# Feed-forward by Strassen's seven products in a split-precision decoder kernel

## The reference, cut to what matters

```python
h = h + jnp.einsum('btnd,de->bte', g * pb, w_out)
u = rmsnorm(h, g_mlp) @ w_up
h = h + jnp.square(jax.nn.relu(u)) @ w_down
h = h + (p_l @ w_ple) * jax.nn.sigmoid(rmsnorm(h, g_ple) @ w_ple_gate)
```

## Time and profile before

| | us |
|---|---|
| median of 3 runs | 2022.32 |
| lowest, highest | 2021.87, 2022.51 |
| span of the profiled execution | 2021.3 |
| product with w_out and feed-forward, in the chain | 1061.4 to 1878.7 |

### The profile page before, as it was taken

How to read it: one execution, slowest core, us unless ns; L and a number is a source line. 1 busy time by engine, 2 the same in 40 slices (tenths; PEclk the granted TensorE clock), 3 DMA queues, 4 the chain that set the end, 5 groups by cost and what they waited for, 6 DMA issues and landing times. The chain is left out here.

```text
span 2021.3 us, 34022 instructions
## 1 busy us (share of the span) xinstructions
PE 1994.1 (99%) x12822; PEld 1961.5 (97%) x12822; DVE 874.8 (43%) x1359; ACT 438.3 (22%) x855; POOL 637.1 (32%) x414
## 2 busy tenths in 40 slices
PE   8999999999999999999999999999999999999997
PEld 7999999999999999999999999999999999999997
DVE  5101443447464655544675543123213311444557
ACT  5112333321111222231232221012002200212312
POOL 2323222222232222224473233232323232323423
PEclk9999999999999999999999999999999999999999
DMA  3441212126443555587553111111111111111313
GB/s 117 136 137 32 57 54 63 58 79 198 121 141 116 172 152 162 164 163 225 179 175 102 53 42 51 43 46 48 44 50 42 52 42 52 42 52 42 105 32 126
DMA packets 239738, 190.35 MB, mean 94 GB/s; under 512 B 17005, under 2 KB 209625, under 8 KB 239268
## 3 DMA queue, kind: packets, MB, share of 16 engines
q1 hardware_dynamic: 224004, 167.03, 28.5%
q10 hardware_dynamic: 15648, 22.13, 3.5%
HBM read 156.05 MB, written 33.09 MB: 94 GB/s over the span
## 5 line engine op out<-in xcount | busy, mean ns | idle before, releaser
L142 PE MATMUL acc<-x_hi,w_hi 128*128 128x344 f32 x2448 | 791.7, 323 | 1.2 <-DVEq L1794 1.2
L142 PE MATMUL acc<-x_hi,w_lo 128*128 128x344 f32 x2448 | 782.8, 320 | 0.0
L142 PE MATMUL acc<-x_lo,w_hi 128*128 128x344 f32 x2448 | 782.0, 319 | 0.0
L112 POOL TENSOR_SCALAR w_hi<-w_raw 128x1024 fp32r<-128x1024 f32 (+1 forms) x174 | 182.0, 1046 | 1176.4 <-PE acc L142 991.5
L142 PEld LDWEIGHTS acc<-x_hi,w_hi 128*128 128x128 f32 x2448 | 460.9, 188 | 2.3 <-issue 1.5
L142 PEld LDWEIGHTS acc<-x_lo,w_hi 128*128 128x128 f32 x2448 | 460.6, 188 | 0.0
L142 PEld LDWEIGHTS acc<-x_hi,w_lo 128*128 128x128 f32 x2448 | 460.5, 188 | 0.0
L115 POOL TENSOR_TENSOR w_lo<-w_raw,w_hi 128x1024 fp32r<-128x1024 f32 (+1 forms) x174 | 407.0, 2339 | 14.5
L142 PE MATMUL acc<-z_hi,w_hi 128*128 128x344 f32 x768 | 246.0, 320 | 0.0
L142 PE MATMUL acc<-z_lo,w_hi 128*128 128x344 f32 x768 | 245.0, 319 | 0.0
L142 PE MATMUL acc<-z_hi,w_lo 128*128 128x344 f32 x768 | 245.0, 319 | 0.0
(11 more groups left out here) (307 smaller groups left out, 2110.1 us busy)
## 6 DMA issues: line engine op xcount, KB each, us to landing
w_raw<-in_w_in SPq DMA_DIRECT2D x64, 512.0 KB, 4.2
page<-in_cache_k SPq DMA_DIRECT2D x64, 256.0 KB, 3.1
page<-in_cache_v SPq DMA_DIRECT2D x64, 256.0 KB, 2.7
w_raw<-in_w_up SPq DMA_DIRECT2D x32, 512.0 KB, 4.0
w_raw<-in_w_down SPq DMA_DIRECT2D x32, 512.0 KB, 4.1
merge_gate<-merge_gates SPq DMA_DIRECT2D x22, 516.0 KB, 3.7
merge_gates<-gate_out ACTq DMA_DIRECT2D x18, 516.0 KB, 3.3
w_raw<-in_w_ple_gate SPq DMA_DIRECT2D x14, 512.0 KB, 4.2
```

Source lines behind the costliest of these rows:

```text
L112: nc.gpsimd.tensor_scalar(k.w_hi[:, par, 0:kb, :], k.w_raw[:, par, 0:kb, :], 1.0, 1.0, ALU.mult, ALU.mult).then_inc(k.w_rounded, 1)
L142: mm = k.nc.tensor.matmul(k.acc[:, c, 0:CW], w[:, par, i, :], x[:, i, cols], start=(i == 0 and j == 0), stop=(i == kb - 1 and j == 2))
```

## The change

The feed-forward's two products are made by Strassen's scheme in its Winograd form. An up *pair* is two blocks of 128 outputs, the two halves of the contraction (even and odd blocks of h) and two halves of 516 columns (`HALF`), each half as two units of 258 (`UNIT`). Seven products replace eight. In a product of an up pair 2 units x 4 tiles x 3 passes = 24 matmuls run; a down pair takes only 4 blocks of u (`DOWN_GROUPS` = 8 groups of 4 pairs), so its products have 12. Seven of the sums that the scheme needs are accumulated in PSUM or added by VectorE.

The operands are new: for the weights GpSimd makes four sums per pair, ScalarE rounds the seven operands (before, GpSimd did), GpSimd makes their low parts. For z the sums are made once (`t_mix`, `t_hi`, `t_lo`); for u per up pair: three quadrants are read and gated with two instructions each, one with one, then squared, four differences are made, and seven operands rounded and split. They are stored in DRAM (`u_rows`) from a buffer of 4 slots in h's upper half and loaded again for the down products; h itself goes to DRAM (`h_back`) and comes back. The sums of squares are multiplied by ones between the first and the second product of pair 0.

```diff
+PRODUCTS = (1, 5, 6, 2, 7, 3, 4)
+    def round_weight(self, act, pair, o):
...
+            act.wait_ge(s["product"], pair.n * NPROD + (o - 2 if o < 3 else -1 if o == 3 else o - 3))
+        k.nc.scalar.activation(self.slot(pair, o, k.w_hi), self.weight_source(pair, o), ACT.Copy).then_inc(s["w_hi"], 1)
+    def split_pair(self, pool, pair):
...
+        nc.gpsimd.tensor_tensor(t0, a21, a22, ALU.add).then_inc(s["sums_ready"], 1)
...
+        nc.gpsimd.tensor_tensor(t1, t0, a11, ALU.subtract).then_inc(s["sums_ready"], 1)
+        for o in range(4):
+            low(o)
+        pool.wait_ge(s["w_lo"], pair.n * NPROD + 2)
+        nc.gpsimd.tensor_tensor(t0, a11, a21, ALU.subtract).then_inc(s["sums_ready"], 1)
+        low(4)
+        pool.wait_ge(s["w_lo"], pair.n * NPROD + 3)
+        nc.gpsimd.tensor_tensor(t1, a12, t1, ALU.subtract).then_inc(s["sums_ready"], 1)
+        low(5)
+        low(6)
+    def multiply(self, pe, pair, o, tiles):
+        pe.wait_ge(s["w_lo"], pair.n * NPROD + o + 1)
+        if j == 2:
+            pe.wait_ge(s["p1"], pair.n + 1)
...
+            pe.wait_ge(s["read"], pair.n * READS + {1: -3, 5: -1, 6: 0, 7: 2, 3: 1, 4: 4}[j])
+        for e in range(2):
+            for i, (b, kt) in enumerate(tiles):
+                hi, lo = (self.ops.rows(j, b, part, kt)[:, 0, e * UNIT:(e + 1) * UNIT] for part in range(2))
+                for step, (w, x) in enumerate(((w_hi, hi), (w_hi, lo), (w_lo, hi))):
...
+    def scalar(self, act):
+        def steady(pair, after):
+            n = pair.n
+            square(n - 1, 3, 2)
+            u_hi(n - 1, 2)
+            self.round_weight(act, pair, 3)
+            keep_p1(n)
+            u_hi(n - 1, 3)
+            self.round_weight(act, pair, 4)
+            u_hi(n - 1, 4)
+            self.round_weight(act, pair, 5)
+            u_hi(n - 1, 5)
+            self.round_weight(act, pair, 6)
+            square(n, 0, 0)
+            u_hi(n - 1, 6)
+            self.round_weight(act, after, 0)
+            square(n, 1, 3)
+            u_hi(n, 0)
+            self.round_weight(act, after, 1)
+            square(n, 2, 1)
+            u_hi(n, 1)
+            self.round_weight(act, after, 2)
...
+    def vector(self, dve):
+        def open_other(n, o, j, other, quad, right, i):
+            dve.wait_ge(s["product"], n * NPROD + o)
+            nc.vector.tensor_tensor(two_units(quads[:, quad, :]), self.read_bank(j), two_units(other), ALU.add)\
+              .then_inc(s["read"], 1)
+            dve.wait_ge(s["read"], n * READS + i + 3)
+            nc.vector.scalar_tensor_tensor(out=quads[:, quad, :], in0=quads[:, quad, :], scalar=0.0,
+                                           in1=rstd[:, token_half(right)], op0=ALU.max, op1=ALU.mult).then_inc(s["opened"], 1)
...
+        def steady(n):
+            open_21(n - 1)
+            mixed(n - 1, 0)
+            mixed(n - 1, 1)
+            u_lo(n - 1, 2)
+            mixed(n - 1, 2)
+            keep_f(n)
+            u_lo(n - 1, 3)
+            keep_u2(n)
+            u_lo(n - 1, 4)
+            open_11(n)
+            u_lo(n - 1, 5)
+            mixed(n - 1, 3)
+            open_22(n)
+            u_lo(n - 1, 6)
+            u_lo(n, 0)
+            open_12(n)
+            u_lo(n, 1)
...
+        def down_pair(pair, previous, extra):
...
+            previous()
...
+            keep_f(n)
+            add_kept(n, 2 * q + 1, 0, P1)
...
+            keep_u2(n)
...
+            add_kept(n, 2 * q + 1, 1, F)
...
+            add_read(n, 4, 2, 2 * q, 0)
...
+            add_kept(n, 2 * q, 1, U2)
...
+            add_read(n, 5, 7, 2 * q + 1, 1)
...
+            add_read(n, 6, 3, 2 * q, 1)
@@ MixOut.sync, for b in range(3, KD) @@
             weights(b)
+            store(b - 3)
@@ Merge.gpsimd, for q in range(NQ) @@
+            if q == KD:
+                pool.wait_ge(k.mlstm_done, 1)
+                k.clear_semaphores(pool, k.decode_sems)
+@@ back_half, sync @@
+            sp.wait_ge(done["product"], ALL * NPROD)
+            sp.wait_ge(done["sq_added"], 4 * OUTS)
```

More of the change, by code:

```diff
@@ L1607 @@
 NQ = len(STEPS)
-BLOCK_PARTS = [(b, slice(0, TT)) for b in range(KD - 1)] + [(KD - 1, cols) for cols in CHUNKS]
-NP = len(BLOCK_PARTS)
 class Merge:
@@ L1934, in back_half @@
[L1934 to L1940 removed]
+        plain_place = ctx.enter_context(ExitStack())
@@ L1953, in back_half @@
         sent = [k.sem(ctx, f"y_sent{i}") for i in range(3)]
-        last = {n: k.sem(ctx, "ld_" + n) for n in ("h_done", "rounded", "split", "squared", "sq_added")}
-        PG = KD * NCH
+        ffn = FeedForward(k, ctx, mix, h, ops, sums, pt, base)
+        done = ffn.s
+        ALL = UPS + DOWN_GROUPS * OUTS
         def emb_bank(u):
@@ L2078, in gates @@
                 if u < 2:
-                    pe.wait_ge(k.acc_free, e0 * NCH + u + 1)
-                    pe.wait_ge(last["split"], NP - 1 + u)
+                    pe.wait_ge(done["read"], (ALL - 1) * READS + 3)
+                    pe.wait_ge(done["z_lo"], 4 * OUTS - 3 + 2 * u)
                 else:
@@ L2083, in gates @@
                 for i in range(KD):
+                    if u < 2 and i == KD - 1:
+                        pe.wait_ge(done["z_lo"], 4 * OUTS)
                     for step, (w, x) in enumerate(((k.w_hi, z_hi), (k.w_hi, z_lo), (k.w_lo, z_hi))):
```

819 lines of the change are left out of this document (653 added, 166 removed).

## The result

The changed kernel takes 2057.66 us (median of 4 runs, 2056.94 to 2058.44) against 2022.41 for the kernel before (4 runs, 2021.87 to 2022.83): ratio 1.0171, 95% interval 1.0157 to 1.0186. It is slower by 35 us, where the forecast was 11 us faster and the range ended at 2056.

The account below looks back on a forecast made before the run. TensorE's own matmuls, busy 99% of the span, were taken as the bound. The feed-forward terms 34 + 348 + 16 + 313 + 4 made 715 us against 726.5, giving 2011 us for the kernel; range 1968 to 2056.

Parts of the forecast that it names:

- TensorE's own work: Feed-forward matmuls: 5,376 of 258 columns at 0.118 us, 634.4 us in all, 90.4 us less (74.8 at the upper bound).
- The up pair: Steady up pairs: 23.2 us each, between 20.4 and 25.3, against 19.8 of TensorE's own work.
- the walk: One steady up pair followed instruction by instruction across ScalarE, GpSimd and VectorE; it repeats at 23.5 us.
- its signs: Up pair: two-SBUF VectorE instructions above 1.2 us mean, PSUM ones 0.70, TensorE idle 3.4 us behind w_lo and VectorE reads.
- The 20.4 us of summed times: Up pair's shared VectorE and GpSimd path: 11 x 1.14 + 14 x 0.56 us, the lower bound for the pair.
- Rival C: Up pairs: TensorE's short stalls repeatedly lower its granted clock, 26 us a pair, +42, total 2053 us; chance 0.10.
- Rival B: Down pairs: GpSimd's hand-over with ScalarE sets them at 11.2 us, total 2046; decides from 10.5 a pair; chance 0.27.
- steady down pairs: Down pairs after the first: 10.1 us each, between 9.9 and 11.2; 31 of them make 313 us.
- At nothing: operand stores and loads: Feed-forward transfers at 205 to 240 GB/s stay covered and cost nothing; cover is gone beyond some 320.
- First down pair: 10 leftover VectorE instructions, +6 (0 to 8): Change from up to down pairs: leftover VectorE work on shared data adds 6 us to the first down pair's 9.9.
- +4 (0 to 9): End of the stage: last quadrant's rounding and low part, and later p and w_ple loads, add 4 us.
- Pair 0: First up pair after w_out, with the sums of squares and a half-clock spell: 34 us, bounds 24 and 42.

Follow-up runs that it names:

- the run with all roundings early: On the kernel with weights 2 and 3 rounded first: all up-pair weight roundings as early as possible, GpSimd's last two sums one low part earlier; 2037.94 us.
- the measured best kernel: Changed kernel with roundings and sums early, leftovers, loads and weights reordered, sums left in the bank for products 3 and 4; 2019.86 us, ratio 0.9986.

## Why the prediction was wrong, by its own steps

**TensorE's own work** was right: 12 matmuls take 1.44 us, 0.120 each, against 0.118 with 0.1208 as the bound, and pairs without a wait take 20.17 and 10.06 (forecast 19.8 and 9.9). The pace that the prediction put at nothing fixed is 0.465 ns a column here, against its 0.457. The Trainium skill (TensorE: Matmul & The Clock Gate, Back-to-back issue gap) gives 110 ns by its formula; the trace is 10 ns above that. TensorE's work fell by 80 us, not 90; the estimate of 80 by the page came out although its times are 10 to 12 ns low at 258 and at 344 columns alike.

**The up pair** was right in size, 23.5 against 23.2 (the walk had said 23.5), and its signs came nearly as put: two-SBUF instructions at 1.18 us, PSUM ones at 0.69, and a pair 3.35 us longer than TensorE's own 20.17 (2.1 of it recorded as idle, all behind GpSimd's w_lo). Its cause is now known better than the prediction had it. Of the 3.35 us, 1.66 go by the order of ScalarE's roundings alone. The rest is the shared path: halving GpSimd's low parts takes all of it away. The 20.4 us of summed times, called a lower bound, was not contradicted and not tested closely either: the best pair with all instructions on the path took 21.85, 21.38 with two taken off, and the one at 20.17 had less work on it. Here the trace agrees with the Trainium skill (SBUF — State Buffer, Who interferes with whom) that one of the two waits while the other holds the path: 1.23 us for a low part beside full GpSimd, 0.81 beside half. It doesn't bear out a lock over the whole recorded time of an instruction: with the least times recorded in these runs, 0.68 us on VectorE and 1.28 on GpSimd, a pair's 14 and 11 instructions would be 23.6 us, and pairs with all of them took 21.85. The prediction's shorter 0.56 and 1.14 fit that.

**Rival C** did not happen: the clock is 1.00 in the steady up stage, with about four waits of at most 0.7 us a pair. Outside of it, it fell to 0.50 each time after a longer wait: after w_out (6.65 us), in pair 0 (3.2), in the first down pairs (5.3, 7.1 and 2.6) and in the last three (2.4 twice), and rose again. **Rival B** did not either: steady down pairs 10.24, below the 10.5 from which it decides. GpSimd's 256-element instructions took 0.80 us on average there, just at the sign named for being wrong, and a pair was still 10.24. The time came out above both rivals' (2046 and 2053), by neither's mechanism.

**The step that failed** is "At nothing: operand stores and loads", together with "First down pair: 10 leftover VectorE instructions, +6 (0 to 8)". The volumes were counted as means over a steady pair or group, 205 to 240 GB/s. At the change of stage they fall on one stretch: group 0's seven loads, group 1's seven loads (14.8 MB together), twelve stores of operands (6.3 MB) and three blocks of weights: 22.6 MB in the 60 us from 1520, 376 GB/s at a share of 1.00. The reload of the residual (2.1 MB) comes behind them, from 1580.8 on. TensorE's work from 1520 to pair 19 would be 19 us of pair 15 and three times 10.06, 49 us; in these the same bytes would need 460 GB/s, more than the 428 of the busiest 5 us read. Bytes over rate alone make only 53 us against these 49; the rest of what the stretch cost is that the work in it waits for transfers in order and doesn't run beside them. The prediction had named a limit itself (cover gone beyond some 320) and not asked it of this stretch. That limit was too low besides, since the earlier trace rows are not the busiest stretch before:

```profile
1052.00:1072.00 20.00, 18.80 (x120) 18.54 (x119) 14.10 (x17) 4.90 (x6) 10.10 (x6) 1.00 0.91 313
...
1054.00:1059.00 5.00, 5.00 (x34) 5.00 (x33) 4.20 (x5) 2.63 (x3) 3.09 (x3) 1.00 1.08 405
```

The stores land late, so ScalarE waits 6.2 and 10.8 us for a free slot, in order, ahead of weight roundings; the chain has two pieces of DMA there, 14.2 and 18.4 us. TensorE's waits behind it then bring the clock to half, with some 14 us of busy TensorE in the four windows of 5 us at 0.50 to 0.57 (an estimate from them: 6 to 7 us lost):

```profile
1543.52 0.63 ACT L2238 ACTIVATE h<-quadrants 128x516 fp32r<-128x516 f32 x1 [6.16 <-DMA feed_forward_operands<-h]
...
1567.28 0.63 ACT L2238 ACTIVATE h<-quadrants 128x516 fp32r<-128x516 f32 x1 [10.77 <-DMA feed_forward_operands<-h]
```

That the volume is the greater part is shown by half the loads (17.0 us less), against five reorderings (from 7.6 us less to 5.5 more). Order is not nothing: moving the leftovers, loads and weights together is the 7.6. The leftovers' own share, the other term here, was never measured alone.

**The last three pairs** were in no term of their own: the low parts of z and the sums of squares of the last group were left in the "+4 (0 to 9)" for the end and never added to VectorE's sum for a down pair. The sum could have been made: 9 instructions of a pair and 8 more, at 0.7 to 1.3 us, are at least 12 us against TensorE's 10. Measured: pairs of 14.5, 13.1 and 14.3 us, 11.7 above the forecast, of which narrowing the sums of squares took 6.0 (7.1 from pair 0 to the end).

**Pair 0** (+3.6), steady down pairs (+3.7) and the end (+3.3) were each forecast a little low, none by itself enough to matter; these three together are over a fifth of the miss. The steady down pair's 0.18 us above 10.06 went with GpSimd's earlier sums, so it was a hand-over, rival B's mechanism at a sixth of its price.

**What stays open.** In the order of the run with all roundings early, four differences of 8 columns did not bring the pair to 20.17 but to 20.87, with 0.92 us spent in each; how the meetings on the path fall is not settled beyond that. The rest of the last three pairs' excess was not taken apart; the granted clock of 0.92 over those 45 us is up to 3.6 us of it (an estimate). Nor were some 11 us lost in pair 0, of which some 4 went with half of GpSimd's low parts (30.9 and 26.9 us for the pair). Moving the sums of the last group off VectorE was not tried.

With every number at its best in one kernel (20.17, 10.06, no waits for transfers) the pairs would take 645 us, and the 17 lost around pair 0 come on top; the measured best kernel is 0.14% faster than before. The change removes 80 us of TensorE's time, and the path, the change of stage and the last group take it back.

## What to carry to other kernels

Take a transfer volume not as a mean over the loop but over the worst stretch between two stages, where the last stores, the first loads, the reloads and the next stage's prefetch meet: divide those bytes by the busiest rate that a trace shows, and if that is longer than the work beside them, the difference is paid at least (here it would have been 4 us). Then ask which in-order engine waits for the last of them, for that cost more here than the difference. Make the engine sums once more for the last group of a stage, with what the epilogue hangs on it. When VectorE and GpSimd both work on SBUF, count each two-SBUF instruction on the shared path, prefer a PSUM operand where the bank is free anyway, and on an in-order engine put what others wait for ahead of what itself waits.

## What the runs showed of the hardware

- The core's 16 DMA engines moved 428 GB/s in the 5 us from 1533 and 412 in the 20 us from 1550, between DRAM and SBUF (405 in 5 us and 313 in 20 before). 7.4 MB less at that load was worth 17.0 us; the quotient is 435 GB/s, but it comes of two single runs. The Trainium skill (DMA: Bandwidth & Descriptors, Specifications) has 435 GB/s as the fabric's ceiling, which no stretch of 5 us read here passes; its lower limit for the HBM, about 358 GB/s a core, was passed in these 20 us, and the measurement decides.
- VectorE's time for the same instructions depends on its neighbour: 20.3 us a pair beside 17.0 us of GpSimd's, 16.8 beside 12.3. Its low parts of 516 columns took 1.23 and 0.81 us on average.
- A VectorE tensor_tensor that writes its sum back into the PSUM bank it reads takes 0.69 us for 516 columns, and the one that reads it there 0.70, beside a busy GpSimd; with two SBUF operands ReLU and scale took 0.98 in the kernel after. A difference of 8 columns with two SBUF operands took 0.92 there.

```profile
L2471 DVE SCALAR_TENSOR_TENSOR quadrants<-n_sums,sq_sum 128x516 f32<-128x516 f32 x10 | 7.0, 696 | 0.3
L2468 DVE TENSOR_TENSOR n_sums<-n_sums,kept_products 128x516 f32<-128x516 f32 x10 | 6.9, 692 | 0.0
```
